# Three near-equal column parts for the large matmuls of a streaming encoder trunk

## The reference

```python
proj = rmsnorm(x, g_mix) @ w_in            # 1024 -> 512 (u_a) + 512 (u_b)
y_a, h_last = s5_mixer(u_a, ...)           # complex state space scan, GELU, z * sigmoid(z @ w_glu)
y_b = pool_mixer(u_b, ...)                 # trailing windows 2/4/8/16, mean minus token, @ w_pool
x = x + concat([y_a, y_b]) @ w_out
hf = rmsnorm(x, g_ffn)
x = x + square(relu(hf @ w_ff1)) @ w_ff2   # 1024 -> 4096 -> 1024
```

## Time and profile before

| | |
|---|---|
| median of 3 runs | 2132.76 us (2132.12 to 2133.49) |
| span of the profiled execution, first to last instruction | 2130.4 us |
| TensorE busy | 2068.2 us, 12888 matmuls |
| weight loads busy | 2032.8 us, 12888 loads |
| VectorE / ScalarE / GpSimd busy | 1079.0 / 447.0 / 212.2 us |
| mean granted TensorE clock | 0.994 |

### The profile page before, as it was taken

How to read it: one execution, slowest core, us unless ns; L and a number is a source line. 1 busy time by engine, 2 the same in 40 slices (tenths; PEclk the granted TensorE clock), 3 DMA queues, 4 the chain that set the end, 5 groups by cost and what they waited for, 6 DMA issues and landing times.

```text
span 2130.4 us, 29080 instructions
## 1 busy us (share of the span) xinstructions
PE 2068.2 (97%) x12888; PEld 2032.8 (95%) x12888; DVE 1079.0 (51%) x1423; ACT 447.0 (21%) x560; POOL 212.2 (10%) x294
## 2 busy tenths in 40 slices
PE   8999899999999999999999999999999999999997
PEld 7888899999999999999999889999999999999997
DVE  7988464455453535353558725643333434343346
ACT  6232431211011111111332234311110101111112
POOL 2253120000000000010110331100000000000002
PEclk9999999999999999999999999999999999999999
DMA  4555111111211112123232641111111111111112
GB/s 172 139 147 165 50 55 50 40 50 40 92 60 51 60 42 70 42 71 122 92 124 80 183 121 38 47 42 48 40 50 40 50 40 50 40 49 41 43 47 84
DMA packets 62493, 152.77 MB, mean 72 GB/s; under 512 B 8576, under 2 KB 21408, under 8 KB 61984
## 3 DMA queue, kind: packets, MB, share of 16 engines
q1 hardware_dynamic: 49552, 112.76, 16.8%
q0 software_dynamic: 9072, 24.65, 4.1%
q10 hardware_dynamic: 3744, 13.50, 1.6%
HBM read 123.36 MB, written 27.53 MB: 71 GB/s over the span
## 4 chain that ended last, share of the span: by engine, by line
PE 87%; DVE 6%; ACT 3%; issue 2%; DMA 1%; POOL 0%; ACTq 0%; DVEq 0%; POOLq 0%
PE tile L509 82%; DVE h_low L1227 2%; PE tile L827 2%; DVE x L1548 1%; ACT h_high L887 1%; DVE w_low L1223 1%; ACT w_high L861 1%; PE small L721 1%; PE small L715 1%; PE small L623 1%; PE small L597 0%; DVE pool_s L1210 0%; POOL y_a L1835 0%; DMA ya_dram<-u_blocks 0%; DMA y_a<-ya_dram 0%
## 5 line engine op out<-in xcount | busy, mean ns | idle before, releaser
L509 PE MATMUL tile<-h_high,w_high 128*128 128x408 f32 (+1 forms) x1920 | 426.9, 330 | 17.1 <-DVE w_low L1223 10.6
L1548 DVE TENSOR_TENSOR x<-tile,x 128x816 f32<-128x816 f32 (+1 forms) x304 | 205.4, 717 | 455.3 <-PE tile L509 445.2
L509 PE MATMUL tile<-h_high,w_low 128*128 128x408 f32 (+1 forms) x1920 | 423.1, 328 | 0.0
L509 PE MATMUL tile<-h_low,w_high 128*128 128x408 f32 (+1 forms) x1920 | 422.8, 328 | 0.0
L509 PEld LDWEIGHTS tile<-h_high,w_high 128*128 128x128 f32 x1920 | 320.9, 188 | 22.0 <-issue 13.5
L509 PEld LDWEIGHTS tile<-h_high,w_low 128*128 128x128 f32 x1920 | 320.4, 188 | 1.1
L509 PEld LDWEIGHTS tile<-h_low,w_high 128*128 128x128 f32 x1920 | 320.2, 188 | 1.0
L509 PE MATMUL tile<-hidden_high,w_high 128*128 128x408 f32 (+1 forms) x1440 | 318.3, 329 | 2.1 <-DVE x L1548 1.2
L509 PE MATMUL tile<-hidden_low,w_high 128*128 128x408 f32 (+1 forms) x1440 | 316.4, 328 | 0.0
L509 PE MATMUL tile<-hidden_high,w_low 128*128 128x408 f32 (+1 forms) x1440 | 316.3, 328 | 0.0
L861 ACT ACTIVATE w_high<-w_raw 128x1024 fp32r<-128x1024 f32 x162 | 170.5, 1052 | 661.4 <-PE tile L509 653.9
(11 more groups left out here) (212 smaller groups left out, 1694.0 us busy)
## 6 DMA issues: line engine op xcount, KB each, us to landing
w_raw<-w_blocks SPq DMA_DIRECT2D x164, 512.0 KB, 3.5
x<-x_t ACTq DMA_DIRECT2D x8, 544.0 KB, 10.8
u_blocks<-ua_dram SPq DMA_DIRECT2D x64, 68.0 KB, 2.7
ya_dram<-u_blocks ACTq DMA_DIRECT2D x8, 544.0 KB, 3.2
y_a<-ya_dram POOLq DMA_DIRECT2D x64, 68.0 KB, 2.7
x_kept<-x ACTq DMA_DIRECT2D x8, 544.0 KB, 2.7
cy_dram<-y_quarter POOLq DMA_DIRECT2D x16, 256.0 KB, 2.9
carry_weights<-cy_dram POOLq DMA_DIRECT2D x8, 512.0 KB, 5.6
```

The costliest lines, as they stand in the source:

```text
L509: mm = pe.matmul(ps[tile][:, c, 0:(b - a) * J], lhs, xt[:, k, a * J:b * J], start=(first and n == 0), stop=(last and n == 2))
L1548: ins = v.tensor_tensor(xt, pt_, xt, ALU.add)
```

## The change

The large products cut their 1088 columns at 364 and 728, not at 408 and 816: the three matmuls of a group are 364, 364 and 360 wide. `halves` follows with pieces of 728 and 360. The pooled channels' tiles are computed by the same `products` with the old cuts (`FRAMES`), and the last stage has code of its own, which is not touched. Layouts in SBUF, weights, waits and transfers stay.

```diff
--- before.py
+++ after.py
@@ -27,7 +27,9 @@
 GP = GROUPS // 2
 EPS = 1e-5
 CHUNKS = ((0, 3), (3, 6), (6, 8))
-WIDE = 3 * J
+EVEN = 364
+THIRDS = ((0, EVEN), (EVEN, 2 * EVEN), (2 * EVEN, T))
+FRAMES = tuple((a * J, b * J) for a, b in CHUNKS)
 
 
 
@@ -332,9 +334,9 @@
 
         def halves(tile, flat, also=()):
 
-            yield (tile[:, 0:2, 0:WIDE], flat[:, 0:2 * WIDE].rearrange("p (c n) -> p c n", c=2),
-                   *(a[:, 0:2 * WIDE].rearrange("p (c n) -> p c n", c=2) for a in also))
-            yield (tile[:, 2, 0:2 * J], flat[:, 2 * WIDE:T], *(a[:, 2 * WIDE:T] for a in also))
+            yield (tile[:, 0:2, 0:EVEN], flat[:, 0:2 * EVEN].rearrange("p (c n) -> p c n", c=2),
+                   *(a[:, 0:2 * EVEN].rearrange("p (c n) -> p c n", c=2) for a in also))
+            yield (tile[:, 2, 0:T - 2 * EVEN], flat[:, 2 * EVEN:T], *(a[:, 2 * EVEN:T] for a in also))
 
         class Steps:
 
@@ -501,21 +503,21 @@
 
         @block.tensor
         def _(pe):
-            def products(tile, slot, col, k, xh, xl, first, last):
+            def products(tile, slot, col, k, xh, xl, first, last, parts=THIRDS):
 
                 for n, (wt, xt) in enumerate(((whi, xh), (whi, xl), (wlo, xh))):
                     lhs = wt[:, slot, col * P:(col + 1) * P]
-                    for c, (a, b) in enumerate(CHUNKS):
-                        mm = pe.matmul(ps[tile][:, c, 0:(b - a) * J], lhs, xt[:, k, a * J:b * J],
+                    for c, (a, b) in enumerate(parts):
+                        mm = pe.matmul(ps[tile][:, c, 0:b - a], lhs, xt[:, k, a:b],
                                        start=(first and n == 0), stop=(last and n == 2))
                 return mm
 
-            def product(tile, slot, col0, n_k, xh, xl, ready=None, backwards=False):
+            def product(tile, slot, col0, n_k, xh, xl, ready=None, backwards=False, parts=THIRDS):
                 order = list(range(n_k))[::-1] if backwards else list(range(n_k))
                 for k in order:
                     if ready:
                         ready(k)
-                    mm = products(tile, slot, col0 + k, k, xh, xl, k == order[0], k == order[-1])
+                    mm = products(tile, slot, col0 + k, k, xh, xl, k == order[0], k == order[-1], parts)
                 mm.then_inc(tile_done, 1)
 
             def tile_at(n):
@@ -658,7 +660,7 @@
                             sum_part(2 * l, 1)
                         if t == 1 and k == 4:
                             sum_part(2 * l, 2)
-                    product(t % 2, t % 2, 0, KD, hhi, hlo, ready)
+                    product(t % 2, t % 2, 0, KD, hhi, hlo, ready, parts=THIRDS if t < KA else FRAMES)
                     if l == 0:
                         if 3 <= t < 7:
                             drives(0, t - 3)
```

## The result

The changed kernel takes 2136.3 us (median of 20 runs, 2133.2 to 2140.5) against 2132.3 us (20 runs of the kernel before, 2128.4 to 2134.1). The ratio is 1.0021, 95% interval 1.0015 to 1.0028: slower by 0.2%, which lies on the very edge of what I had called no change. The profiled execution of it took 2138.5 us with a span of 2136.7, 6.3 more than the span before.

The account below looks back on a forecast made before the run. The prediction took TensorE's matmul stream, at about 497 ns per group of three, to bound the kernel. It summed 2132.8 + 0 (TensorE) + 0 (readers), rounded to 2133 us, range 2116 to 2147.

Parts of the forecast that it names:

- The stream sets the time.: Whole kernel: TensorE's matmul stream sets the time; 3298 groups of three large matmuls, so 1 ns per group is 3.3 us.
- Widths on a straight line, so even parts give nothing back.: Large products on TensorE: price linear in width, 0.449 ns per column, so three parts of 1088 columns cost the same.
- I take the straight line, 0.: TensorE term of the sum: the new cuts change the group price by 0.
- bounds of -3.1 and +3.6: Group price on TensorE, ns: ends from lines through the cheapest and dearest last-stage rows, -10.2 and +11.9 us in all.
- a group that stays at 496 to 498 ns: Large products' trace: start-to-start step of a group inside a tile expected after the change.
- the new starts cost more: Rival, large products: the second part's start at byte 1456 slows the stream to 500.1 ns per group, 2145 us; slower 0.30.
- nothing to see: Large products: the change only reorders columns, so the time stays the same within 0.2%; this is the forecast; chance 0.38.
- the narrow part hides a stall: Rival, 272-wide matmul: next weight load lacks room; even parts give about 491 ns, 2115 us; faster, cheap end included, 0.32.
- The load's floor priced at nothing: Weight loads on TensorE: 109 ns per load and matmul leaves a 272-wide step of 124 ns 15 ns to spare; 0.
- The readers' sum unchanged: VectorE's two reads of a full tile: 912 and 522 ns, together 1434 as before; ScalarE's likewise; 0.
- The 16-byte lines: SBUF starts: by the skill's unit of fast reads, 1456 = 91 x 16 is as good a start as any.
- the slower rival: Large products: the rival that new part starts cost more, 2145 us, chance 0.30; said to fall by the 16-byte rule.

Follow-up runs that it names:

- e1: Changed kernel with the second part reading from column 360 instead of 364, widths 364, 364, 360 kept: 2131.7 us, ratio 0.9996.
- e2: Changed kernel put back to widths 408, 408, 272, with the second part reading from column 404: 2142.6 us, ratio 1.0051.
- e13: Kernel before the change with w_high and w_low moved 128 bytes further on, cuts as before: 2143.1 us, ratio 1.0051.
- e9: Changed kernel with cuts at 360 and 720 instead of 364 and 728, nothing left out: 2125.5 us, ratio 0.9972.
- e6: Changed kernel with cuts at 448 and 896 instead of 364 and 728: 2198.4 us, ratio 1.0309.
- e10: Changed kernel with the second part reading from column 361 instead of 364, widths 364, 364, 360 kept: 2151.6 us, ratio 1.0090.
- e4: Changed kernel with cuts at 384 and 768 instead of 364 and 728: 2133.1 us, ratio 1.0005.
- e5: Changed kernel with widths 364, 364, 360 read from columns 0, 320 and 704, every start a multiple of 256 bytes: 2139.9 us, ratio 1.0035.
- e15: As e5, with w_high and w_low also moved 128 bytes further on: 2173.1 us, ratio 1.0192.
- e3: Changed kernel with cuts at 368 and 736 instead of 364 and 728: 2132.7 us, ratio 1.0010.

## Why the prediction was right, and where its sum was off

- *The stream sets the time.* Right. 3298 groups times the measured 1.7 ns makes 5.6 us; the profiled spans differ by 6.3, the medians by 4.0, the ratio says 4.5.
- *Widths on a straight line, so even parts give nothing back.* Right as far as widths go. Sets of 408-408-272, 384-384-320 and, from e1, 364-364-360 all cost 496.7 to 496.8.
- *"I take the straight line, 0."* This is the term that was mis-sized. The starts were outside the line, and measured +1.7 ns, inside the bounds of -3.1 and +3.6. With it the sum would have been about 2138 us.
- *Some of it was luck.* The forecast was a group that stays at 496 to 498 ns. The mean of 498.4 lies near that, but hardly any stretch of the stream does: most went up by one step of 3.3 ns and a fifth went down by one, and the two cancel in part. Had the whole stream gone to 500.0, as in e2 and e13, the change would have cost 3.3 x 3298 = 11 us (an estimate), and come to about 2143 us; e2 and e13 came to 2142.6 and 2143.1. That the bounds of -3.1 and +3.6 nearly match the two paces is not something the sum had a reason for.
- *The rival "the new starts cost more"* had the right place, and nearly the right size in three quarters of the stream; in the mean it had half. I gave it 3.6 ns and 2145 us. The measured ratio of 1.0021 is just past the border of 0.2% between the two cases, so of "nothing to see" and "the new starts" it is the second that happened, at its smallest. I had given them 0.38 and 0.30. The clue was in the rows: z at 500.0 in the earlier trace rows, which I used for the size, though not for what it means. A second clue was misread. I held against this rival that the parts at byte 3264 "are the cheapest of their width", but every 272-wide matmul of the earlier trace rows starts there, those at 126.4 ns as well as those at 123.4. What differs between them is the weight buffer, and moving it in e13 closed the gap.
- *The rival "the narrow part hides a stall"* is wrong as a mechanism. The changed kernel has no narrow part, and most of its groups start 500 ns apart. Groups faster than 496.5 exist, in a fifth of its stream and in most of e9's, but e1 has the same even widths and none of them: the starts decide.
- *The load's floor priced at nothing.* Right, since no part here is narrow enough; e6 shows the floor at the 109 ns that was read from the transposes.
- *The readers' sum unchanged.* Right: 912 and 522 were forecast, 914 and 522 measured.
- *The 16-byte lines.* e10, off such a line, cost 6.3 ns more than e1. That agrees, in one run, with the Trainium skill's page "SBUF — State Buffer" (the SBUF cachelines note). But the start at 1456 bytes, on a line, cost 1.7 ns more than the one at 1440, so the conclusion that the slower rival falls by this rule is refuted.

What stays open: which starts and widths are cheap, and why the paces lie 3.3 ns apart. The parts' distances from the weights, modulo 256 bytes, were 128, 224 and 64 before, 128, 48 and 224 after, 128, 32 and 224 in e1, 128, 32 and 192 in e9, and 128, 128 and 128 in both e4 and e5. I have no formula that orders them, and e9's gain was found and not forecast. Nor do I know what chooses between the two paces of the chain after the change, 60.19 or 59.41 us for the same 360 matmuls. Each kernel has one trace, so it is open too whether an execution always takes the same pace at the same place. The changed kernel's runs spread over 7 us, before's over 6 in 20 runs, which says little. That the weight reads and the column reads get in each other's way in SBUF is inferred from e13 and e15; the runs show only that their addresses count in relation to each other.

## What to carry to other kernels

Before balancing the widths of matmuls in a stream, find at least three widths, or two and a mixed group, and look whether their prices lie on a line (two alone always do). If they do, mostly starts and floors are left to matter; here the floor was the 109 ns step of the small transposes. When matmuls are the bound, treat the byte address of each part, relative to the weights loaded beside it, as a tuning knob (e9 to e15 span 2.2% here). Scan cuts in steps of 4 and 8 columns, and try a shift of the weight buffer. Look at the price stretch by stretch before you average it: a mean that looks unchanged can be a fast and a slow pace in one execution (e3). Where one input of the same shape runs at another price, as z did, ask for its address first.

## What the runs showed of the hardware

- Two operands of TensorE influence each other by address. With widths 364, 364, 360 and weights and all three parts at the same residue modulo 256 bytes, a group costs 508 to 513 ns, with 128 bytes between them 499 (e5, e15). With widths 384, 384, 320 the same residues cost 500.0 (z in e4). The Trainium skill's page "SBUF — State Buffer" (Who interferes with whom) gives TensorE two independent read ports, one for each operand; by that the weights' address should not matter, and here it moved the time from 2139.9 to 2173.1 us.
- The stream runs at paces 3.3 ns apart per group of three: 493.3, 496.7, 500.0 or 503.3 ns, and can change between them in one execution (94.96 and 96.22 us for the same 576 matmuls in e3).
- A 4-byte shift of one start costs 6.3 ns in 497 (e10 against e1), a 16-byte shift 1.7 to 3.1 on the mean (changed kernel, e2).
- The spacing of weight loads of 128 columns has a floor of 108 to 109 ns (e6, transposes), though each is shown as 188 ns long. A 192-wide matmul makes the one behind it wait (e6), a 272-wide one does not; by the straight line the border would lie near 236 columns, (109 - 3.2)/0.4485, an estimate that no run tries.
